# Odd mixer's softmax rows in four buffers: scores and maxima ahead of turning the slot behind, and the normalising ahead of two waits

## The reference

```python
isc = jnp.where(key_pos <= t, isc, NEG)          # index scores, 256 keys kept
_, sel = lax.top_k(isc, n_sel)
logit = jnp.einsum('bchd,bckhd->bhck', qc, ksel) * scale + bias
logit = jnp.where(valid, logit, NEG)
p = jax.nn.softmax(logit, axis=-1)
yd = jnp.einsum('bhck,bckhd->bchd', p, vsel)
```

## Time and profile before

| | |
|---|---|
| median of 3 runs | 2037.86 us (2030.65 to 2037.87) |
| the profiled execution's own time | 2036.56 us |
| its span in the trace | 2034.8 us |
| PE busy | 1988.3 us, 98% of the span |
| DVE busy, ACT busy | 1079.5 us (53%), 772.5 us (38%) |
| even mixer | about 386 to 613 us of the span |
| odd mixer | about 1336 to 1676 us; its pairs 4 to 6 from 1473 to 1610, pair 7 from 1610 to 1647 |

### The profile page before, as it was taken

How to read it: one execution, slowest core, us unless ns; L and a number is a source line. 1 busy time by engine, 2 the same in 40 slices (tenths; PEclk the granted TensorE clock), 3 DMA queues, 4 the chain that set the end, 5 groups by cost and what they waited for, 6 DMA issues and landing times.

```text
span 2034.8 us, 25407 instructions
## 1 busy us (share of the span) xinstructions
PE 1988.3 (98%) x9054; PEld 1626.9 (80%) x9054; DVE 1079.5 (53%) x1673; ACT 772.5 (38%) x1110; POOL 50.0 (2%) x86
## 2 busy tenths in 40 slices
PE   7999999999989999999999999999999899999999
PEld 5888888888778888888888888877777678888887
DVE  4443444677674444446434444657877754444444
ACT  4322223467763222224322222455455653222232
POOL 1000000000000000000000000011110000000000
PEclk9999999999999999999999999999999899999999
DMA  4254423321122332333333232376754343322233
GB/s 168 95 125 123 135 95 102 104 73 63 54 72 93 96 101 93 97 99 114 93 97 99 93 100 96 103 188 148 167 124 104 77 130 93 100 97 93 101 95 103
DMA packets 60863, 213.80 MB, mean 105 GB/s; under 512 B 6616, under 2 KB 6872, under 8 KB 60792
## 3 DMA queue, kind: packets, MB, share of 16 engines
q1 hardware_dynamic: 52080, 184.97, 28.1%
q0 software_dynamic: 6192, 22.55, 6.0%
q10 hardware_dynamic: 2520, 5.36, 1.4%
HBM read 185.32 MB, written 4.72 MB: 93 GB/s over the span
## 4 chain that ended last, share of the span: by engine, by line
PE 87%; DVE 6%; ACT 4%; issue 2%; DMA 0%; SPq 0%; DVEq 0%; ACTq 0%
PE ps_unit L527 28%; PE ps_unit L529 28%; PE ps_unit L528 28%; DVE cv L1722 1%; DVE pt_lo L1482 1%; PE ps_s L527 1%; ACT probs L1012 1%; PE ps_y L527 0%; DVE probs L1458 0%; ACT w_hi L904 0%; PE ps_misc L617 0%; PE ps_y L528 0%; PE ps_y L529 0%; ACT L919 0%; PE ps_t L656 0%
## 5 line engine op out<-in xcount | busy, mean ns | idle before, releaser
L527 PE MATMUL ps_unit<-xs_hi,w_hi 128*128 128x512 f32 x1768 | 699.1, 395 | 12.3 <-DVE xs_lo L1297 11.3
L904 ACT ACTIVATE w_hi<-raw 128x1024 fp32r<-128x1024 f32 x301 | 319.2, 1061 | 1025.9 <-PE ps_unit L529 1010.9
L528 PE MATMUL ps_unit<-xs_lo,w_hi 128*128 128x512 f32 x1768 | 691.2, 391 | 0.0
L529 PE MATMUL ps_unit<-xs_hi,w_lo 128*128 128x512 f32 x1696 | 662.6, 391 | 0.0
L1289 DVE TENSOR_TENSOR w_lo<-raw,w_hi 128x1024 fp32r<-128x1024 f32 x301 | 368.2, 1223 | 85.3 <-ACT w_hi L904 85.3
L527 PEld LDWEIGHTS ps_unit<-xs_hi,w_hi 128*128 128x128 f32 x1768 | 333.4, 189 | 89.3 <-DVE w_lo L1289 9.1
L528 PEld LDWEIGHTS ps_unit<-xs_lo,w_hi 128*128 128x128 f32 x1768 | 333.6, 189 | 69.1 <-issue 1.7
L529 PEld LDWEIGHTS ps_unit<-xs_hi,w_lo 128*128 128x128 f32 x1696 | 320.2, 189 | 67.6
L527 PE MATMUL ps_unit<-a_hi,w_hi 128*128 128x512 f32 x892 | 353.2, 396 | 4.6 <-DVE w_lo L1289 2.2
L528 PE MATMUL ps_unit<-a_lo,w_hi 128*128 128x512 f32 x892 | 350.1, 392 | 0.0
L529 PE MATMUL ps_unit<-a_hi,w_lo 128*128 128x512 f32 x845 | 330.0, 391 | 0.0
(11 more groups left out here) (215 smaller groups left out, 1299.5 us busy)
## 6 DMA issues: line engine op xcount, KB each, us to landing
raw<-w_stream_dram SPq DMA_DIRECT2D x344, 512.0 KB, 3.5
w_lo<-raw POOLq DMA_DIRECT2D x28, 512.0 KB, 5.0
w_lo_3rd<-raw POOLq DMA_DIRECT2D x15, 512.0 KB, 5.0
skew<-table ACTq DMA_DIRECT2D x1, 2560.0 KB
bias_t<-skew ACTq DMA_DIRECT2D x1, 2048.0 KB, 9.4
out_dram<-xt SPq DMA_DIRECT2D x8, 256.0 KB, 2.0
xt<-xt_in_dram SPq DMA_DIRECT2D x7, 256.0 KB, 6.5
bd_raw<-bd_in_dram SPq DMA_DIRECT2D x1, 512.0 KB, 8.3
```

Of the source, the lines that this page charges most:

```text
L527: pe.matmul(ps, lhs_hi, rhs_hi, start=first, stop=False)
L528: pe.matmul(ps, lhs_hi, rhs_lo, start=False, stop=False)
L529: return pe.matmul(ps, lhs_lo, rhs_hi, start=False, stop=last)
L904: act.activation(w_hi[:, s, :], raw[:, slot, :], ACT.Copy).then_inc(w_hi_done, 1)
```

## The change

- In the odd mixer (`a >= 4`) rows lie in four buffers: `probs` and a new `probs_more`, and the maxima, sums and their inverses have four columns. A row waits until row `R-4` has been turned, where it waited for row `R-2`. `probs_more` takes the place of `ki_hi` and `ki_lo`, which aren't used any more by then.
- On PE, odd mixer: `score(a, p)` goes ahead of the two `turn`s, and in slot 3 `weigh(a, 0)` goes behind them.
- On DVE, odd mixer: `row_bias` of a slot's two rows goes ahead of the two `pt_low`.
- On DVE, both mixers, iterations 1 to 3, slots 2 and 3: `attend_end` (the two `row_norm`) goes ahead of `pair_in` (`head_inv`, `v_low`). In `mix_out` it was there already.

No instruction is added or removed.

```diff
--- before.py
+++ after.py
@@ -159,9 +159,9 @@
         hstd = sb("hstd", [P, 16])
         hinv = sb("hinv", [P, 2, 16])
         probs = sb("probs", [P, 2, T])
-        negmax = sb("negmax", [P, 2])
-        rowsum = sb("rowsum", [P, 2])
-        rowinv = sb("rowinv", [P, 2])
+        negmax = sb("negmax", [P, 4])
+        rowsum = sb("rowsum", [P, 4])
+        rowinv = sb("rowinv", [P, 4])
         pt_hi = sb("pt_hi", [P, 14, P], F32R)
         pt_lo = sb("pt_lo", [P, 14, P], F32R)
 
@@ -188,6 +188,7 @@
         relu = [probs[:, 0, :], probs[:, 1, :]]
         c_pad = [sb(f"c_pad{j}", [P, T + DW_TAPS - 1])[:, :] for j in range(4)]
         cv = [sb(f"cv{j}", [P, T])[:, :] for j in range(4)]
+        probs_more = sb("probs_more", [P, 2, T], at=top[0])
         ki_hi = sb("ki_hi", [P, T], F32R)
         ki_lo = sb("ki_lo", [P, T], F32R)
         branch_sum = c_pad[0][:, 0:T]
@@ -376,6 +377,14 @@
 
             return ps_misc[:, :] if (j, which) == (3, 1) else ps_y[:, :]
 
+        def row_of(a, R):
+
+            return (probs_more if a >= 4 and R // 2 % 2 else probs)[:, R % 2, :]
+
+        def turned_before(a, R):
+
+            return R - 3 if a >= 4 else R - 1
+
         def pair_step(it, u):
 
             return u if ODD_SLOTS[it] == 5 or u < 4 else 9 - u
@@ -653,7 +662,7 @@
                 if R >= 2:
                     pe.wait_ge(pt_lo_done, R - 1)
                 for j in range(r // 2 + 1):
-                    mm = pe.transpose(ps_t[:, R % 2, j * P:(j + 1) * P], probs[:, R % 2, j * P:(j + 1) * P], ident[:, :])
+                    mm = pe.transpose(ps_t[:, R % 2, j * P:(j + 1) * P], row_of(a, R)[:, j * P:(j + 1) * P], ident[:, :])
                 mm.then_inc(turned_done, 1)
 
             def weigh(a, half):
@@ -680,13 +689,17 @@
 
                 if p == 0 and not first:
                     weigh(a - 1, 1)
-                if p == 3:
+                if p == 3 and a < 4:
                     weigh(a, 0)
+                if p < 4 and a >= 4:
+                    score(a, p)
                 for r in (2 * p - 2, 2 * p - 1):
                     if r >= 0:
                         turn(a, r)
-                if p < 4:
+                if p < 4 and a < 4:
                     score(a, p)
+                if p == 3 and a >= 4:
+                    weigh(a, 0)
 
             def lru_gate(j, which):
                 if which == 0:
@@ -1000,16 +1013,16 @@
                 act.wait_ge(score_done, R + 1)
                 act.wait_ge(hinv_done, a + 1)
                 if R >= 2:
-                    act.wait_ge(turned_done, R - 1)
-                act.activation(probs[:, R % 2, 0:n], ps_s[:, R % 2, 0:n], ACT.Copy,
+                    act.wait_ge(turned_done, turned_before(a, R))
+                act.activation(row_of(a, R)[:, 0:n], ps_s[:, R % 2, 0:n], ACT.Copy,
                                scale=hinv[:, a % 2, c:c + 1]).then_inc(scaled_q_done, 1)
 
             def exp(a, r):
 
                 R, n = 8 * a + r, (r // 2 + 1) * P
                 act.wait_ge(biased_done, R + 1)
-                p = probs[:, R % 2, 0:n]
-                act.activation(p, p, ACT.Exp, scale=-1.0, bias=negmax[:, R % 2:R % 2 + 1], accum_out=rowsum[:, R % 2:R % 2 + 1]).then_inc(exp_done, 1)
+                p = row_of(a, R)[:, 0:n]
+                act.activation(p, p, ACT.Exp, scale=-1.0, bias=negmax[:, R % 4:R % 4 + 1], accum_out=rowsum[:, R % 4:R % 4 + 1]).then_inc(exp_done, 1)
 
             def pt_high(a, r):
                 R, n = 8 * a + r, r // 2 + 1
@@ -1450,28 +1463,28 @@
 
                 R, h, t = 8 * a + r, r % 2, r // 2
                 n = (t + 1) * P
-                p = probs[:, R % 2, 0:n]
+                p = row_of(a, R)[:, 0:n]
                 if on_dve(a, r):
                     c = r
                     dve.wait_ge(score_done, R + 1)
-                    dve.wait_ge(turned_done, R - 1)
+                    dve.wait_ge(turned_done, turned_before(a, R))
                     dve.scalar_tensor_tensor(p, ps_s[:, R % 2, 0:n], hinv[:, a % 2, c:c + 1], keep(t), ALU.mult,
                                              ALU.add).then_inc(masked_done, 1)
                 dve.wait_ge(*scores_read(a, r))
                 if R == 0:
                     dve.wait_ge(bias_landed, 16)
                 if R >= 2:
-                    dve.wait_ge(exp_done, R - 1)
+                    dve.wait_ge(exp_done, turned_before(a, R))
                 dve.tensor_tensor_reduce(p, p, bias_t[:, 2 * (a % 4) + h, T - n:T], -1.0, 3e38, ALU.add, ALU.min,
-                                         negmax[:, R % 2:R % 2 + 1]).then_inc(biased_done, 1)
+                                         negmax[:, R % 4:R % 4 + 1]).then_inc(biased_done, 1)
 
             def row_norm(a, r):
                 R, n = 8 * a + r, (r // 2 + 1) * P
-                p, inv = probs[:, R % 2, 0:n], rowinv[:, R % 2:R % 2 + 1]
+                p, inv = row_of(a, R)[:, 0:n], rowinv[:, R % 4:R % 4 + 1]
                 dve.wait_ge(exp_done, R + 1)
                 if R >= 2:
                     dve.wait_ge(prob_done, R - 1)
-                dve.reciprocal(inv, rowsum[:, R % 2:R % 2 + 1]).then_inc(rowinv_done, 1)
+                dve.reciprocal(inv, rowsum[:, R % 4:R % 4 + 1]).then_inc(rowinv_done, 1)
                 dve.wait_ge(rowinv_done, R + 1)
                 dve.tensor_scalar(p, p, inv, None, ALU.mult).then_inc(prob_done, 1)
 
@@ -1490,10 +1503,13 @@
             def attend(a, p, first):
                 if p == 0 and not first:
                     y_low(a - 1)
+                if p < 4 and a >= 4:
+                    row_bias(a, 2 * p)
+                    row_bias(a, 2 * p + 1)
                 for r in (2 * p - 2, 2 * p - 1):
                     if r >= 0:
                         pt_low(a, r)
-                if p < 4:
+                if p < 4 and a < 4:
                     row_bias(a, 2 * p)
                     row_bias(a, 2 * p + 1)
 
@@ -1663,8 +1679,10 @@
                             split_lo(n + 2, (n + 2) % RAW, (n + 2) % 2)
                         if it:
                             attend(it - 1, u, it == 1)
+                        if it and u in (2, 3):
+                            attend_end(it - 1, u)
                         pair_in(it, u)
-                        if it:
+                        if it and u not in (2, 3):
                             attend_end(it - 1, u)
                         lru(it - 1, u, n)
                 mix_out(i, 3)
@@ -1871,8 +1889,10 @@
                             attend(4 + it - 1, u, it == 1)
                         if u == 1 and it in (1, 2):
                             conv_low(it + 1)
+                        if it and u in (2, 3):
+                            attend_end(4 + it - 1, u)
                         pair_in(4 + it, pair_step(it, u))
-                        if it:
+                        if it and u not in (2, 3):
                             attend_end(4 + it - 1, u)
                         if it == 3 and u in (1, 2):
                             conv_norm(u + 1)
```

## The result

| | before | changed |
|---|---|---|
| profiled execution | 2036.56 us, span 2034.8 | 2020.63 us, span 2018.8 |
| median, first comparison (5 runs each) | 2032.29 us (2030.65 to 2037.87) | 2020.63 us (2015.30 to 2022.54) |
| ratio, first comparison | | 0.9924, 95% interval 0.9910 to 0.9938 |
| ratio, second comparison (17 and 5 runs) | | 0.9919, 95% interval 0.9905 to 0.9933 |

The kernel became 0.8% faster, about 15.5 us of 2036 by the first ratio and 16.5 us by the second, each within 3 us. The medians alone differ by 11.7 us in the first comparison and by 19.0 us in the second, since single runs of the kernel before spread over more than 8 us (2030.65 to 2039.28); the two ratios agree, and the text goes by them. The forecast was 12.4 us by its sum, 11 us with the allowance that it added.

What follows compares the result with a forecast made beforehand. PE, busy for 98% of the span, was taken as the bound, with DVE nearly a second one in places. Gains summed to 12.4 us: 2036.56 to 2024.2, plus 1.3 for the runs' median, 2025.5 us; range 2018 to 2034.

Steps and rivals of the forecast that it cites:

- the allowance: Whole kernel: 1.3 us added to the forecast time, as the runs' median lay that far above the profiled execution.
- forecast A: Whole kernel: the forecast itself, 2025.5 us, with its own range 2021 to 2030; chance 0.52.
- Term 4: Pair 6 slot 0, layer norm's mean: DVE 6.2 us earlier, PE 4.35, so the 1.46 us wait goes; gain 1.5 us.
- rival B: Pairs 4 to 6: fewer waits also raise PE's clock, 6.9 us back, 2018.6 us; chance 0.15.
- Scores ahead of turns: PE, odd mixer: scores fill idle time at turns; gain 0.7 us in pair 4 slot 2, 0.5 in pair 7 slot 1.
- Slot 4 of pairs 4 and 5: Odd mixer: normalised rows come earlier, so PE's waits at these turns go; gain 1.9 + 1.75 us.
- Pair 6: Slots 1 to 4: the turn's 4.27 us wait goes and layer norm's scalings start earlier; gain 4.5 us, bounds 1.0 and 5.4.
- The even mixer: Pairs 0 and 1: normalising fills DVE's wait at `v_lo`, removing two 0.75 us waits of `weigh`; gain 1.5 us.
- Rival C: Pair 6: layer norm's chain holds it, leaving 8.4 us, or 6.9 (2031 us) if the mean's gain fails too; chance 0.20.
- Rival E: Whole kernel slower: turns delayed by the scores ahead pass that on, 2046.5 us, or 2050 with clock falls; chance 0.08.

Runs made afterwards that it cites:

- second comparison: The changed kernel run again, unchanged, against the kernel before: 2017.45 us, ratio 0.9919 (0.9905 to 0.9933).

## Where the prediction held, and which steps failed

The mechanism held: rows ready earlier, PE's waits for them down from 11.2 to 1.3 us (2.1 in the second profile), DVE's wait at `hinv` 0.64 us (the prediction named 0.6), `v_lo` without a wait in pairs 4 and 5, and the clock over 1473 to 1610 not lower (0.93, 0.96 and 0.92 in the windows of the earlier trace rows). The size was short: the change is measured at 15.5 to 16.5 us against 12.4 in the sum, or 11.1 with the allowance, and the changed kernel's 2020.63 us lie 4.9 us under the forecast of 2025.5, inside the wide range but just under forecast A's own (2021 to 2030).

Two steps failed. Term 4 has the wait at the mean of the layer norm go, with 1.5 us gained. The wait stayed, at 1.75 us, and nothing was gained there: PE came 6.7 us earlier and not 4.35, and DVE only 6.4. And the sum puts the clock at nothing, leaving it to rival B with a chance of 0.15; it gave PE 1.45 us in pair 5, which went into the wait at the mean, 1.6 us in the even mixer, and a part of pair 6.

The first failure alone hardly moves the total, which up to the mean was 6.4 us against 5.85 forecast. What made the forecast short is 0.55 us there, 0.8 us in pair 6, 0.8 us of waits and 1.6 us of clock in the even mixer, 3.7 us together, and the allowance of 1.3 us.

1. *Scores ahead of turns.* 0.7 and 0.5 us forecast, 0.8 and 0.45 in the ledger.
2. *Slot 4 of pairs 4 and 5.* 1.9 and 1.75 us forecast. 2.4 in pair 4. In pair 5 it was 3.55: the wait of 1.75, 0.35 of small pieces, and 1.45 because the unit behind `head_ssq` ran wholly at 2.4 GHz. This last is part of rival B. It came each time, and was spent at the mean.
3. *The mean.* 1.5 us forecast, none gained: the step whose mechanism failed. The term compared DVE's gain of 6.2 us with PE's of 4.35 and found 0.4 us in hand. DVE's was right: the mean's addition came 10.2 us earlier, 6.4 of them within the odd mixer. PE's was 6.7 us, by pair 5's clock and the small pieces. Up to the mean the forecast has 0.7 + 1.9 + 1.75 + 1.5 = 5.85 us and the ledger 6.4. Whichever way PE gets its time, at this place it can't have more than DVE gives. Taking two taps of 0.77 us away from DVE there cut the wait by 1.56 us, which shows it. With PE's old order the stretch at 1.2 GHz in pair 5 is back, and the wait is 0.85 us. As an estimate, without pair 5's clock PE would have come 6.7 - 1.45 = 5.25 us earlier, and the mean would have given 6.4 - 5.25 = 1.15 us.
4. *Pair 6.* 4.5 us forecast, 5.3 measured: 1.5 up to the variance (the short waits of two turns went too, which the term left out), 0.7 from there to slot 3, 0.5 lost in it, 3.6 behind it. In the 3.6 the clock has a part that the term didn't have: the turn and `spread_k` of slot 4 took 1.84 and 1.92 us before, at a clock of 0.72, and 1.04 and 1.13 us in the changed kernel, at 1.00, 1.6 us together. That `spread_k` would wait for `v_lo` was named as a sign against the forecast; it came here, at 0.76 us, but as a remainder of 4.27 us and not as a new price, and not in the second profile. `v_lo` waited 1.13 us in this pair, over the 0.3 us that the prediction named, also in the first profile only.
5. *The even mixer.* 1.5 us forecast, 2.3 measured by waits (2.3 to 2.4 in the kernel with that edit alone). All of the wait of 0.75 us at `weigh` was gained, and some 0.4 us around it, in each of two pairs. Of these, 0.12 us are `weigh` and the scores behind it (455.37 to 458.79, and 454.68 to 457.98), which ran closer together; the rest is spread over gaps that no row shows as a wait.
6. *The allowance.* 1.3 us were added since the median of three runs stood above the profiled execution. With 17 runs the median of before is 2036.44 us (2036.05 and 2035.7 in the two other comparisons), that execution's own time within 1 us; it should not have been added.

Without the even mixer's clock, which came by chance, the ledger is 16.0 - 1.6 = 14.4 us, beside 12.4 forecast. Pair 5's 1.45 us isn't to be taken off as well, since by the estimate above the mean would have given it back. Up to 1.6 us of the 14.4 are again the clock, in slot 4 of pair 6; how much of that would have been waited for anyway isn't shown. Rival B, which spoke of pairs 4 to 6, was thus true of the clock, but of its 6.9 us at most these 1.6 reached the time. Rival C was right on the mean and wrong on the layer norm's chain. Rival E asked for turns that come later; none did. What stays open is why pair 5 keeps its clock and pair 4 doesn't. The order of scores and turns alone isn't the reason: the kernel with the normalising alone has PE's old order and keeps it (1.00 from 1530 to 1542), the one with all but PE's order loses it (0.86).

## What to carry to other kernels

When a wait on one engine is filled, the gain downstream is the filling engine's gain, not the sum of the waits of the engine that waits: add up both, and take the smaller at each place where they meet. A stretch at the lower clock can hide a wait that the same engine would have at full clock, so read a wait, or its absence, with the granted clock of the stretch ahead of it. And scores, or whatever else feeds the slowest engine, belong ahead of the work that waits for it: here that order was worth about 4 of the 12.1 us of the odd mixer, with the buffers that allow it.

## What the runs showed of the hardware

- The stretches at 1.2 GHz behind `head_ssq` (16 matmuls of 2 columns) made the unit behind it 1.4 to 2.8 us longer (7.2 and 8.6 us where it is 5.8 at the full clock). In repeated executions of one kernel they stood in nearly the same places (before) or in others (changed), with the same time in total within 0.3 us in the odd mixer. The Trainium skill (TensorE: Matmul & The Clock Gate, Part 1: The HAM clock gate) says that the gate's phase isn't set by the program, so that its changes move from run to run; the changed kernel's two profiles agree with that, those of before don't show it.
- A stretch at the lower clock and a wait behind it can stand for each other. In one kernel (before), pair 6, `head_ssq` took 3.55 us with 0.72 us of wait behind it, or 1.93 us with 3.17 us, and the stretch from the variance to slot 3 was 6.00 us both times. Between kernels, in pair 4, they came as clock 0.79 and no wait (1504.53), and as clock 1.00 and 2.06 us (1503.08), with 43.4 and 43.0 us for the pair.
